# GpSimd makes the low parts of six of the 23 weight granules of each expert half

## The reference, cut to what matters

```python
top_vals, top_idx = lax.top_k(logits, TOP_K)                 # 2 of 8 experts for each token
gates = jnp.sum(jax.nn.one_hot(top_idx, N_EXPERTS) * softmax(top_vals)[..., None], axis=1)
for e in range(N_EXPERTS):                                   # D_MODEL 1024, D_FF_EXPERT 1792
    out = out + gates[:, e:e + 1] * ((silu(t @ w_gate[e]) * (t @ w_up[e])) @ w_down[e])
```

## Time and profile before

| | |
|---|---|
| median of three runs | 1334.85 us |
| the profiled execution: time, span of its trace | 1333.65 us, 1331.9 us |
| PE busy | 1231.1 us, 92% of the span |
| DVE busy | 919.5 us, 69% |
| ACT busy | 772.3 us, 58% |
| POOL busy | 20.8 us, 2% |
| memory read | 294.45 MB, 222 GB/s over the span |
| steady part of the expert stage, 832 to 1248 us | PE 416.0 of 416 us busy, DVE 379.6 us, ACT 329.6 us, POOL none |

### The profile page before, as it was taken

One profiled execution on the slowest core, in us unless ns is written; L12 is line 12 of the kernel. 1 busy time (PEld: TensorE's weight loads), 2 busy tenths in 40 slices (PEclk: granted clock), 3 DMA queues, 4 the chain that ended last, 5 costly groups with the idle time before them and its releaser, 6 DMA issues.

```text
span 1331.9 us, 16189 instructions
## 1 busy us (share of the span) xinstructions
PE 1231.1 (92%) x5901; PEld 1043.2 (78%) x5901; DVE 919.5 (69%) x1160; ACT 772.3 (58%) x1022; POOL 20.8 (2%) x65
## 2 busy tenths in 40 slices
PE   4999998889999969999998887999999999999984
PEld 4877787768888858877786677888888888888873
DVE  5467466655544444576566586899989998999984
ACT  4555565535333325445664456877787778777861
POOL 3000000000000000000000000000000000000000
PEclk9999999999999979999998988999999999999996
DMA  9545423466555325536224519999999999999960
GB/s 319 189 145 188 160 88 110 135 238 228 183 187 188 130 79 182 174 127 191 101 88 131 181 46 356 354 328 351 341 351 331 351 339 350 334 352 337 372 234 33
DMA packets 120382, 296.53 MB, mean 223 GB/s; under 512 B 9028, under 2 KB 33632, under 8 KB 119792
## 3 DMA queue, kind: packets, MB, share of 16 engines
q1 hardware_dynamic: 118720, 288.66, 62.6%
q0 software_dynamic: 1584, 6.88, 1.5%
HBM read 294.45 MB, written 1.05 MB: 222 GB/s over the span
## 4 chain that ended last, share of the span: by engine, by line
PE 83%; DVE 7%; ACT 5%; issue 3%; DMA 1%; POOL 0%; SPq 0%; DVEq 0%; POOLq 0%; ACTq 0%
PE bank L1183 25%; PE bank L1185 25%; PE bank L1184 25%; ACT w_hi L526 2%; DVE w_lo L794 2%; PE bank L1451 1%; DVE proj L898 1%; PE bank L1354 1%; PE bank L1334 1%; PE bank L1474 1%; PE bank L1229 1%; DMA raw<-in_w_in 1%; PE bank L1468 1%; PE bank L1469 1%; DVE w_lo L999 1%
## 5 line engine op out<-in xcount | busy, mean ns | idle before, releaser
L999 DVE TENSOR_TENSOR w_lo<-raw,w_hi 128x896 fp32r<-128x896 f32 (+1 forms) x368 | 407.0, 1130 | 61.9 <-ACT w_hi L667 55.0
L667 ACT ACTIVATE w_hi<-raw 128x896 fp32r<-128x896 f32 (+1 forms) x368 | 357.2, 985 | 130.6 <-PE bank L1185 128.0
L794 DVE TENSOR_TENSOR w_lo<-raw,w_hi 128x1536 fp32r<-128x1536 f32 (+3 forms) x147 | 246.9, 1686 | 221.9 <-ACT w_hi L526 221.7
L1183 PE MATMUL bank<-w_hi,aT_hi 128*128 128x512 f32 (+2 forms) x848 | 334.7, 395 | 20.9 <-DVE aT_lo L817 7.8
L1185 PE MATMUL bank<-w_hi,aT_lo 128*128 128x512 f32 (+2 forms) x848 | 327.4, 386 | 0.0
L526 ACT ACTIVATE w_hi<-raw 128x1536 fp32r<-128x1536 f32 (+4 forms) x147 | 209.1, 1427 | 203.5 <-PE bank L1185 196.6
L1184 PE MATMUL bank<-w_lo,aT_hi 128*128 128x512 f32 (+2 forms) x848 | 326.6, 385 | 0.0
L1183 PEld LDWEIGHTS bank<-w_hi,aT_hi 128*128 128x128 f32 x848 | 162.0, 191 | 49.5 <-DVE aT_lo L817 9.7
L1185 PEld LDWEIGHTS bank<-w_hi,aT_lo 128*128 128x128 f32 x848 | 161.5, 190 | 27.4
L1184 PEld LDWEIGHTS bank<-w_lo,aT_hi 128*128 128x128 f32 x848 | 161.9, 191 | 25.0
L1183 PE MATMUL bank<-w_hi,bT_hi 128*128 128x448 f32 (+1 forms) x384 | 147.4, 384 | 6.0 <-DVE v L920 4.0
(11 more groups left out here) (217 smaller groups left out, 995.0 us busy)
## 6 DMA issues: line engine op xcount, KB each, us to landing
raw<-in_moe_w_gate SPq DMA_DIRECT2D x128, 448.0 KB, 4.9
raw<-in_moe_w_up SPq DMA_DIRECT2D x128, 448.0 KB, 4.9
raw<-in_moe_w_down SPq DMA_DIRECT2D x112, 512.0 KB, 5.9
raw<-in_w_in SPq DMA_DIRECT2D x40, 768.0 KB, 4.4
raw<-in_dense_w_gate SPq DMA_DIRECT2D x22, 512.0 KB, 3.9
raw<-in_dense_w_up SPq DMA_DIRECT2D x22, 512.0 KB, 4.8
raw<-in_dense_w_down SPq DMA_DIRECT2D x11, 1024.0 KB, 4.9
raw<-in_w_in SPq DMA_DIRECT2D x20, 512.0 KB, 4.6
```

The source lines that it names most:

```text
L667: act.activation(w_of(hi_slot, i), raw_of(i), ACT.Copy).then_inc(e_hi_made, 1)
L794: dve.tensor_tensor(w_lo[:, j, 0:n], raw[:, b % 2, j, 0:n], w_hi[:, j, 0:n].bitcast(F32), ALU.subtract).then_inc(lo_made[j], 1)
L999: dve.tensor_tensor(w_of(lo_slot, i), raw_of(i), w_of(hi_slot, i).bitcast(F32), ALU.subtract).then_inc(e_lo_made, 1)
L1183: pe.matmul(dst, x_hi, b_hi, start=start, stop=False)
```

## The change

`POOL_LO` names six granules of the 23: n = 2, 6, 10 and 14 of the gate and up granules, and 18 and 21 of the down granules. In every step but step 0 GpSimd makes their low parts, by the same subtraction on the same tiles (`split_granules`), behind the same wait for ACT's copy. DVE passes over them. They have a semaphore of their own, `e_lo_pool`, and `LO_COUNT` holds how many granules of the same engine there are up to granule i, so that SP (in front of a load) and PE (in front of a granule) wait on the one engine or on the other. In steps 1 to 15 there are six such granules each, and in step 16 two: 92 of the 368 that run.

```diff
+POOL_LO = (2, 6, 10, 14, 18, 21)
+BY_POOL = [n in POOL_LO and (r, k) != (r, 0) for r, k, n in GRANULES]
+LO_COUNT = [sum(BY_POOL[j] == BY_POOL[i] for j in range(i + 1)) for i in range(len(GRANULES))]
...
+        def wait_split(eng, i):
+
+            eng.wait_ge(e_lo_pool if BY_POOL[i] else e_lo_made, LO_COUNT[i])
...
-                                sp.wait_ge(e_lo_made, RAW_BEFORE[i] + 1)
+                                wait_split(sp, RAW_BEFORE[i])
...
+            def split_granules(r):
+                for i in range(PER_ROUND * r, PER_ROUND * (r + 1)):
+                    if BY_POOL[i]:
+                        pool.wait_ge(e_hi_made, i + 1)
+                        pool.tensor_tensor(w_of(lo_slot, i), raw_of(i), w_of(hi_slot, i).bitcast(F32), ALU.subtract).then_inc(e_lo_pool, 1)
+
+            split_granules(0)
+            second_round(pool, split_granules)
             norm_root(4, None)
...
-                    if i + W_SLOTS < PER_ROUND * (r + 1):
+                    if i + W_SLOTS < PER_ROUND * (r + 1) and not BY_POOL[i + W_SLOTS]:
                         expert_lo(i + W_SLOTS)
...
-                pe.wait_ge(e_lo_made, i + 1)
+                wait_split(pe, i)
```

More of the change, by code:

```diff
@@ L271, in build_trunk @@
         e_raw_in = [sem(f"e_raw_in{s}") for s in range(RAW_SLOTS)]
+        e_lo_pool = sem("e_lo_pool")
         e_hi_made, e_lo_made, e_used, e_silu_made, e_hid_made, e_hid_tr, e_hT_hi_made, e_hT_lo_made = (sem(n) for n in (
```

## The result

| | before | after |
|---|---|---|
| median (range), four runs each | 1334.9 us (1332.63 to 1337.57) | 1346.2 us (1345.99 to 1347.51) |
| ratio after / before, 95% interval | | 1.0086 (1.0066 to 1.0106) |
| profiled execution: time, span | 1333.65 us, 1331.9 us | 1345.99 us, 1344.3 us |

The change makes the kernel slower by 11.3 us, which is clear of noise. The forecast was slower, 1366 us; the loss is about a third of the 32 us that I gave.

A forecast was written before the change was run, and what follows sets the result against it. PE bounds the kernel at 31.9 us a half; under exclusion DVE and GpSimd would need 34.1 us, +33 us, less 1 us at the stage's end: +32 us on 1333.65 us gives 1366 us, range 1331 to 1415 us.

The forecast's parts named there:

- What bounds the kernel: Steady expert stage: PE, busy all 416 us, sets the pace at 31.9 us a half; relieving DVE gains only margin.
- What leaves DVE: Each half: six subtractions, 6.8 us, leave DVE's 29.1 us; 22.3 us stay and 9.6 us would be free.
- What comes to GpSimd: Each half: six subtractions, two streams at 1.07 ns a column plus 0.2 us fixed, 13.3 us (ends 5.8 and 19.3).
- Full exclusion: Steady part: when both engines want to read two SBUF tiles, one stands still until the other is through; chance 0.58.
- a third, 1.5 us: Each half: of DVE's 4.5 us of PSUM work, 1.5 us overlap GpSimd, giving 34.1 us, 2.2 us over PE's 31.9.
- +33 us: Steady part: forecast loss from 2.2 us over in each half, times 15.3 halves.
- The fit: Rival, steady part: GpSimd's work finds DVE's free and PSUM time, PE stays the bound, 1332 to 1334 us; chance 0.29.
- The end of the stage: PE's 8.0 us wait for the last hidden values' low part shrinks as DVE is relieved: -1 us, bounds -1.7 and +3.5.
- The start: Start of the stage: PE's 7.2 us wait hangs on a load and ACT's work behind it, not DVE: 0.
- the loads: SP's loads, waiting for GpSimd's granules, can be issued 1 us later, but ACT never waited for one: 0.
- the flag: GpSimd's flag load and branch behind its last subtraction; its root isn't wanted until over 15 us later: 0.
- the clock: Rival: gaps in PE's work lower its granted clock to 0.98, +10 us on 490 us of PE work, inside the range.

The follow-up runs named there:

- the run with the six on top: Against the kernel before: VectorE makes all 23 low parts and GpSimd makes its six once more into an unread scratch tile; 1456.21 us, ratio 1.091.
- the run with three granules: The changed kernel with GpSimd making the low parts of three granules of 23 (2, 10, 18) instead of six; 1333.95 us, ratio 1.0007 against the kernel before.
- the order changed: The changed kernel with VectorE's low part of the hidden values ahead of the weight's low part, not behind it; 1344.04 us, ratio 1.0069 against the kernel before.

## Why the prediction was wrong

- **What bounds the kernel, and that DVE's relief is worth nothing in the steady part: right.** Nobody makes the six low parts, and PE stays at 416.0 of 416 us.
- **What leaves DVE, 6.8 us of a half: right.** Without the six, 379.6 us fell to 300.4 in 13.04 halves, 6.1 us: the 0.7 us are the overlap of neighbours. The 22.3 us that stay were 23.0.
- **What comes to GpSimd, 2.12 and 2.39 us: right.** Unheld ones took 2.12 and 2.41 us. That it fits so well is in part luck: the same rule with one stream gives 1.16 us for the copy of 896 columns, which took 0.94. The estimate by the Trainium skill, 1.97 and 2.25 us (GPSIMD Engine Reference, section 3.1, Elementwise), is 7% below the traces.
- **Full exclusion as the likelier end: right**, shown by the run with the six on top. The Trainium skill's rule (SBUF — State Buffer, section Who interferes with whom) agrees with these traces: for two tiles on both sides, for DVE's PSUM work, which stayed at its length, for memsets, and for the copy that reads one tile, which held DVE in the seven places where it met it for longer than 0.13 us. What I had left out of the rule is that it excepts VectorE's 2-port modes from what it says of one SBUF input. DVE's sel operation reads one SBUF tile, and it was held: 1553 ns beside a GpSimd subtraction against 276 ns, in the run with three granules. No run here shows in which mode it ran.
- **The step that failed: "So I take a third, 1.5 us: 22.3 + 13.3 - 1.5 = 34.1 us, 2.2 us over, 15.3 times".** The 1.5 us were to be all of GpSimd's time that costs DVE nothing. In the mean of the halves 2 to 15 it was 4.8 us: 2.1 us beside DVE's other work, 1.5 us beside an idle DVE, which the sum had put at nothing, and 0.2 us for each of the six subtractions. The holds were 8.5 us for a half, 1.4 us for each GpSimd subtraction, and the sum has 11.8. With 8.5 the same sum gives 22.3 + 8.5 = 30.8 us, under 31.9 and so no loss at all, and that is wrong too.
- **The second part of the same step, one mean half taken 15.3 times.** I had divided 416 us by 13.04 and taken every half as the mean, 31.9 us on PE and 29.1 us on DVE. In fact PE's halves last from 30.1 to 33.0 us and DVE's work in them from 27.7 to 30.6 us, with a margin from 1.9 us (halves 5, 9, 13, 15) to 4.7 us (half 2), and the holds go from 5.9 to 11.2 us. The forecast's +33 us became +11.0: six halves at nothing, four at 1.6 to 2.9 us, three at 1.0 us, two at 0.1 to 0.2 us. "The fit", my rival, was found in six to eight of the halves and missed in the others. The halves 5, 9 and 13, at 33.6 to 33.7 us, are near my 34.1, but that is luck: their holds are 9.2 to 9.5 us instead of 11.8, DVE's own work in them is 1 us above the mean, and work has shifted into them from the half before (half 4 would have 27.9 - 6.8 + 8.7 = 29.8 us of DVE and has 28.9; half 5 would have 32.8 and has 33.6).
- **What the sum had no term for: the order on DVE.** The halves 6 and 10 lost 1.0 us each with DVE idle for 2.7 us in them, through one wait of PE for a small instruction behind a held subtraction. With the order changed they lost nothing.
- **What gives a half its holds** is what GpSimd meets there, by the rows of the table. The margin alone doesn't order them: the halves 3, 7 and 11 have 2.3 us of it and the shortest holds, half 2 has the most and long ones. What in the order of steps makes GpSimd meet 4.1 us of DVE's other work in one half and 0.3 us in another was not tried.
- **The end of the stage, "I take -1": wrong in sign.** The relief by itself is -1.6 us (8.0 to 6.4, nobody). Under exclusion it measured +2.0 us, inside the +3.5 I had as a bound.
- **The start, the loads, the flag, the clock: right.** The waits at the start are 6.6 us against 7.2, no line has ACT waiting for a DMA, GpSimd's root came when DVE's sums were there, and the clock stayed at 1.00 in the steady part.

## What to carry to other kernels

A subtraction of two SBUF tiles moved from VectorE to GpSimd does not leave VectorE: there it took off 1.1 us and put back 0.85 to 1.9 us, the more the less idle VectorE was, because the two engines took turns. Before such a move, ask whether the relieved engine bounds the stage at all; where it has a margin, the move can only use it up. Take that margin for each repetition and not from the mean of many, and look at what stands behind a held instruction: two halves lost 1 us each with VectorE idle for 2.7 us in them. Memsets on GpSimd did not hold the subtractions. Short copies cost nothing here, but they met few of the subtractions, and seven of these they held. And before an experiment is read as "this doesn't interfere", look whether the two ran at the same time at all. What was worth having lay in the slot map at the end of the stage, in a wait that the same profile showed.

## What the runs showed of the hardware that I had not expected

- A VectorE subtraction of two SBUF tiles that met a GpSimd subtraction came almost wholly behind it. In the changed kernel and in the run with six on top, in each of the halves 2 to 15, the holds, GpSimd's time beside VectorE's PSUM work and its time beside an idle VectorE add up to 11.8 to 12.3 us of GpSimd's 13.3.
- GpSimd's copy with one SBUF input (0.94 us for 896 columns when it meets nobody) and VectorE's subtraction held each other where they met for longer than 0.13 us: 1.17 to 1.18 us and 1.30 to 1.31 us, seven times.
- GpSimd's writes alone (two memsets, 847 ns each) left that subtraction at 1091 ns, with 57 of the narrow ones beside a memset. VectorE's small sel operation (one SBUF tile of 128 columns in, SBUF out, 276 ns) was held by all three: 280 to 951 ns beside memsets (mean 608), 470 and 483 ns beside copies, 1553 ns twice and 2148 ns once beside subtractions. In the changed kernel none of the eight in the steady part met GpSimd's work, and they took 276 ns.
